# Norm sums as one column per token tile: root and reciprocal on four columns, spread over the partitions by products with the identity

## The reference

```python
def _rmsnorm(x, g):
    xf = x.astype(jnp.float32)
    y = xf * lax.rsqrt(jnp.mean(xf * xf, axis=-1, keepdims=True) + EPS)
    return (y * g.astype(jnp.float32)).astype(x.dtype)
...
        h = _rmsnorm(x, norm_g[l, 0]) * (1.0 + sc0) + sh0
        x = x + 0.5 * g0 * _swiglu(h, ffn_w_gate[l, 0], ffn_w_up[l, 0], ffn_w_down[l, 0])
        h = _rmsnorm(x, norm_g[l, 1]) * (1.0 + sc1) + sh1
...
        h = _rmsnorm(x, norm_g[l, 2]) * (1.0 + sc2) + sh2
```

## Time and profile before

| | us |
|---|---|
| median of 3 runs | 3887.87 |
| the runs | 3886.22, 3887.87, 3887.95 |
| profiled execution | 3886.95 |
| its span | 3885.2 |
| TensorE busy | 3486.6 (90%) |
| VectorE busy | 2174.4 (56%) |
| GpSimd busy | 1606.3 (41%) |
| ScalarE busy | 1216.5 (31%) |

### The profile page before, as it was taken

One profiled execution on the slowest core, in us unless ns is written; L12 is line 12 of the kernel. 1 busy time (PEld: TensorE's weight loads), 2 busy tenths in 40 slices (PEclk: granted clock), 3 DMA queues, 4 the chain that ended last, 5 costly groups with the idle time before them and its releaser, 6 DMA issues. The chain is left out here.

```text
span 3885.2 us, 41685 instructions
## 1 busy us (share of the span) xinstructions
PE 3486.6 (90%) x13886; PEld 2361.7 (61%) x13886; DVE 2174.4 (56%) x4271; ACT 1216.5 (31%) x2225; POOL 1606.3 (41%) x960
## 2 busy tenths in 40 slices
PE   6999999899999999999999999897778778777777
PEld 4888676688878887766788876663333333333332
DVE  6546257433326455466333265478677777667664
ACT  3332226443323323145333233432222222222221
POOL 3446330244545455210444632335444444444442
PEclk9999999999999999999999999998998998999998
DMA  6526320122435454200223421269999999999996
GB/s 243 194 95 259 110 98 1 45 97 97 166 126 184 146 201 179 98 17 16 88 97 112 179 82 49 93 255 408 421 422 421 421 421 422 421 421 421 420 420 275
DMA packets 141434, 839.57 MB, mean 216 GB/s; under 512 B 15824, under 2 KB 16464, under 8 KB 63952
## 3 DMA queue, kind: packets, MB, share of 16 engines
q0 software_dynamic: 73728, 536.90, 33.5%
q1 hardware_dynamic: 67536, 300.56, 21.5%
HBM read 835.31 MB, written 2.10 MB: 216 GB/s over the span
## 5 line engine op out<-in xcount | busy, mean ns | idle before, releaser
L256 POOL TENSOR_TENSOR wlo<-wraw,whi 128x1024 fp32r<-128x1024 f32 x357 | 906.2, 2543 | 1462.9 <-ACT whi L252 1462.6
L252 ACT ACTIVATE whi<-wraw 128x1024 fp32r<-128x1024 f32 x357 | 377.4, 1058 | 663.4 <-DMA wraw<-in_wts 371.8
L263 PE MATMUL f_ps<-f_hh,whi 128*128 128x512 f32 x1408 | 550.3, 391 | 0.9 <-DVE f_hl L352 0.9
L264 PE MATMUL f_ps<-f_hl,whi 128*128 128x512 f32 x1408 | 548.2, 389 | 0.0
L265 PE MATMUL f_ps<-f_hh,wlo 128*128 128x512 f32 x1408 | 548.1, 389 | 0.0
L1967 PE MATMUL g_psF<-g_low,g_diagb 128*128 128x512 f32 x660 | 327.6, 650 | 101.0 <-ACT g_diagb L2025 100.9
L1967 PE MATMUL g_psF<-g_own,g_diagb 128*128 128x512 f32 x576 | 279.8, 636 | 71.9 <-ACT g_diagb L2025 71.9
L521 DVE TENSOR_TENSOR f_a<-f_sg,f_ps 128x512 f32<-128x512 f32 x88 | 60.5, 688 | 503.6 <-PE f_ps L265 487.1
L1967 PE MATMUL g_psF<-g_top,g_diagb 128*128 128x512 f32 x524 | 261.8, 651 | 72.3 <-ACT g_diagb L2025 72.2
L1967 PEld LDWEIGHTS g_psF<-g_low,g_diagb 128*128 128x128 f32 x660 | 134.7, 208 | 288.9 <-issue 288.9
L2019 ACT ACTIVATE g_dotb<-g_dotb 128x4 f32<-128x4 f32 (+1 forms) x134 | 27.5, 205 | 898.4 <-DVE g_dotb L2109 898.4
(11 more groups left out here) (400 smaller groups left out, 6396.9 us busy)
## 6 DMA issues: line engine op xcount, KB each, us to landing
wraw<-in_wts SPq DMA_DIRECT2D x360, 512.0 KB, 3.3
m_wrow<-in_ada SPq DMA_DIRECT2D x52, 1024.0 KB, 6.8
m_erow<-in_ada SPq DMA_DIRECT2D x28, 1024.0 KB, 5.0
p_wt<-in_wtok SPq DMA_DIRECT2D x2, 3168.0 KB, 10.5
p_wt<-in_w SPq DMA_DIRECT2D x2, 3072.0 KB, 9.7
g_low<-in_uv,idx POOLq DMA_INDIRECT x165, 24.8
g_own<-in_uv,idx POOLq DMA_INDIRECT x144, 24.3
g_top<-in_uv,idx POOLq DMA_INDIRECT x131, 24.8
```

The source lines that it names most:

```text
L252: self.nc.scalar.activation(self.T.whi[:, j % 4], self.T.wraw[:, j % 2], ACT.Copy).then_inc(self.M["w_hi"], 1)
L256: self.nc.gpsimd.tensor_tensor(self.T.wlo[:, j % 4], self.T.wraw[:, j % 2], self.T.whi[:, j % 4].bitcast(F32), ALU.subtract).then_inc(self ...
L263: self.nc.tensor.matmul(out, hi, xh, start=first, stop=False)
L264: self.nc.tensor.matmul(out, hi, xl, start=False, stop=False)
```

## The change

The sums are turned round: the squares, 128 tokens at a time, are the stationary operand, and one column of the ones is the moving one. Four products give [128, 4]: token t*128+p has its mean square on partition p, column t. The root and the reciprocal are made on these four columns, in `T.root` and `T.inv`, which are unused columns of `T.eps`. `widen` then copies each of the four columns 128 times along the free dimension, in two copies of 256 columns, to the place of the old `T.rstd`, and `spread` multiplies these by the identity, four products of 128 columns, so that the [128, 512] form stands in a PSUM bank, `T.psN`. `norm_split` and its likes read that bank in place of `T.rstd`.

```diff
+def token_sums(nc, T, out, x, first, last):
+    for t in range(TT):
+        mm = nc.tensor.matmul(out[:, t:t + 1], x[:, t * P:(t + 1) * P], T.const[:, C_ONES:C_ONES + 1],
+                              start=first and t == 0, stop=last and t == TT - 1, skip_group_check=True)
+    return mm
+
+def widen(nc, T, dve, sem):
+    nc.vector.reciprocal(T.inv[:, :], T.root[:, :]).then_inc(sem, 1)
+    dve.wait_ge(sem, 1)
+    wide = T.wide[:, :].rearrange("p (t m) -> p t m", t=TT)
+    for a in range(2):
+        nc.vector.tensor_copy(wide[:, 2 * a:2 * a + 2], T.inv[:, 2 * a:2 * a + 2].unsqueeze(2).to_broadcast([P, 2, P])
+                              ).then_inc(sem, 1)
+
+def spread(nc, T, pe, sem, out):
+    for t in range(TT):
+        pe.wait_ge(sem, t // 2 + 2)
+        mm = nc.tensor.matmul(out[:, t * P:(t + 1) * P], T.wide[:, t * P:(t + 1) * P], T.const[:, C_IDENT:C_IDENT + P],
+                              start=True, stop=True, skip_group_check=True)
+    return mm
...
     def total(self, pe):
-        ones = self.T.const[:, C_ONES:C_ONES + P]
         pe.wait_ge(self.M["n_acc"], KD - 2)
-        self.nc.tensor.matmul(self.ps, ones, self.acc, start=True, stop=False)
+        token_sums(self.nc, self.T, self.ps, self.acc, True, False)
         pe.wait_ge(self.M["n_sq"], KD)
...
     def root(self, act):
         act.wait_ge(self.M["n_sum"], 1)
-        self.nc.scalar.activation(self.T.rstd[:, :], self.ps, ACT.Sqrt, ...
+        self.nc.scalar.activation(self.T.root[:, :], self.ps[:, 0:TT], ACT.Sqrt, ...
...
@@ norm_split
-                nc.vector.scalar_tensor_tensor(u[:, k % slots], T.xT[:, k], gain[:, k:k + 1], T.rstd[:, :],
+                nc.vector.scalar_tensor_tensor(u[:, k % slots], T.xT[:, k], gain[:, k:k + 1], T.psN[:, :],
...
@@ ffn
                 Q.total(pe)
-                keep_busy(nc, T, pe, psD[:, 0], 9, 256)
+                keep_busy(nc, T, pe, psD[:, 0], 4, P)
+                Q.spread(pe)
+                keep_busy(nc, T, pe, psD[:, 0], 4, 256)
...
@@ out_proj (and second_mix alike)
-                keep_busy(nc, T, pe, ps[:, 0], 4)
+                keep_busy(nc, T, pe, ps[:, 0], 4, P)
+                Q.spread(pe)
+                keep_busy(nc, T, pe, ps[:, 0], 4, 256)
```

More of the change, by code:

```diff
@@ L173, in _ @@
                 act.wait_ge(M["m_ch"], 3)
[L174 removed]
+                nc.scalar.activation(T.root[:, :], psN[:, 0:TT], ACT.Sqrt, bias=T.eps[:, 0:1]).then_inc(M["n_root"], 1)
                 for n in range(3):
@@ L190, in _ @@
                     pe.wait_ge(M["n_sq"], k + 1)
-                    nc.tensor.matmul(psN[:, :], T.const[:, C_ONES:C_ONES + P], sq[:, k % 2], start=k == 0,
-                                     stop=k == KD - 1).then_inc(M["n_sum"], 1)
+                    token_sums(nc, T, psN, sq[:, k % 2], k == 0, k == KD - 1).then_inc(M["n_sum"], 1)
+                spread(nc, T, pe, M["n_rstd"], psN)
                 pe.wait_ge(M["m_dot"], 2 * ROWS)
-                keep_busy(nc, T, pe, psN, 2)
+                keep_busy(nc, T, pe, psB, 2)
             @block.vector
@@ L207, in _ @@
                         dve.wait_ge(M["n_root"], 1)
-                        nc.vector.reciprocal(T.rstd[:, :], T.rstd[:, :]).then_inc(M["n_rstd"], 1)
+                        widen(nc, T, dve, M["n_rstd"])
                     dve.wait_ge(M["m_row"][j], 16)
@@ L318, in total, with spread @@
     def total(self, pe):
-        ones = self.T.const[:, C_ONES:C_ONES + P]
         pe.wait_ge(self.M["n_acc"], KD - 2)
-        self.nc.tensor.matmul(self.ps, ones, self.acc, start=True, stop=False)
+        token_sums(self.nc, self.T, self.ps, self.acc, True, False)
         pe.wait_ge(self.M["n_sq"], KD)
-        self.nc.tensor.matmul(self.ps, ones, self.sq[:, (KD - 1) % 2], start=False, stop=True).then_inc(self.M["n_sum"], 1)
+        token_sums(self.nc, self.T, self.ps, self.sq[:, (KD - 1) % 2], False, True).then_inc(self.M["n_sum"], 1)
     def root(self, act):
         act.wait_ge(self.M["n_sum"], 1)
-        self.nc.scalar.activation(self.T.rstd[:, :], self.ps, ACT.Sqrt, bias=self.T.eps[:, 0:1]).then_inc(self.M["n_root"], 1)
+        self.nc.scalar.activation(self.T.root[:, :], self.ps[:, 0:TT], ACT.Sqrt, bias=self.T.eps[:, 0:1]).then_inc(self.M["n_root"], 1)
     def rstd(self, dve):
         dve.wait_ge(self.M["n_root"], 1)
-        self.nc.vector.reciprocal(self.T.rstd[:, :], self.T.rstd[:, :]).then_inc(self.M["n_rstd"], 1)
+        widen(self.nc, self.T, dve, self.M["n_rstd"])
+    def spread(self, pe):
+        spread(self.nc, self.T, pe, self.M["n_rstd"], self.T.psN)
+def token_sums(nc, T, out, x, first, last):
[16 more added lines that the diff above has]
+    return mm
 N_SEMS = "n_u n_hi n_lo "
@@ L404, in ffn @@
         psD = ctx.enter_context(nc.psum_tensor("f_psD" + str(which), [P, 2, S], F32))
-        psN = ctx.enter_context(nc.psum_tensor("f_psN" + str(which), [P, S], F32))
         W = Stream(nc, T, M, layer * LAYER_T + (FFN_T + PROJ_T + OUT_T if which else 0))
-        Q = Sums(nc, T, M, a32[:, 0], sg, psN[:, :])
+        Q = Sums(nc, T, M, a32[:, 0], sg, T.psN)
         norm = (nc, T, M, sg, hh, hl, gain, shift)
@@ L1237, in out_proj @@
         ps = ctx.enter_context(nc.psum_tensor("o_ps", [P, 4, S], F32))
-        psN = ctx.enter_context(nc.psum_tensor("o_psN", [P, S], F32))
-        Q = Sums(nc, T, M, acc[:, :], sq, psN[:, :])
+        Q = Sums(nc, T, M, acc[:, :], sq, T.psN)
         with nc.Block() as block:
@@ L1503, in _ @@
                     pe.wait_ge(M["l_sq"], k + 1)
-                    nc.tensor.matmul(psT[:, 0], ones, sg[:, k % 2], start=k == 0, stop=k == KD - 1).then_inc(M["l_sum"], 1)
-                keep_busy(nc, T, pe, psT[:, 1], 4)
+                    token_sums(nc, T, psT[:, 0], sg[:, k % 2], k == 0, k == KD - 1).then_inc(M["l_sum"], 1)
+                keep_busy(nc, T, pe, psT[:, 1], 4, P)
+                spread(nc, T, pe, M["l_r"], T.psN)
+                keep_busy(nc, T, pe, psT[:, 1], 4, 256)
             @block.scalar
@@ L1610, in _ @@
                 act.wait_ge(M["l_sum"], KD)
-                nc.scalar.activation(T.rstd[:, :], psT[:, 0], ACT.Sqrt, bias=T.eps[:, 1:2]).then_inc(M["l_root"], 1)
+                nc.scalar.activation(T.root[:, :], psT[:, 0, 0:TT], ACT.Sqrt, bias=T.eps[:, 1:2]).then_inc(M["l_root"], 1)
             @block.gpsimd
@@ L1778, in _ @@
                 dve.wait_ge(M["l_root"], 1)
-                nc.vector.reciprocal(T.rstd[:, :], T.rstd[:, :]).then_inc(M["l_r"], 1)
+                widen(nc, T, dve, M["l_r"])
         clear(nc, M)
@@ L2193, in build @@
             T.rstd = cw.enter_context(nc.sbuf_tensor("rstd", [P, S], F32))
+            T.wide = T.rstd
+            T.root, T.inv = T.eps[:, 4:8], T.eps[:, 8:12]
             first_block(nc, T)
```

29 lines of the change are left out of this document (17 added, 12 removed).

## The result

The changed kernel takes 3900.42 us, median of 8 runs (3899.04 to 3902.98); the kernel before, on the same chip, 3886.68 us, median of 8 (3883.54 to 3889.91). The ratio is 1.0037, 95% interval 1.0028 to 1.0046: slower, by 13.7 us. The forecast was 3885.0, with a range up to 3892. The profiled run of after took 3901.13 with a span of 3898.6, 13.4 more than before's 3885.2. TensorE is busy for 3519.6 us of it, before for 3486.6.

What follows compares the result with a forecast made beforehand. TensorE, busy 90% of the span, was taken as the bound, its fills holding the barrier at norms. Six norms 2.6, second_mix 0.3 + 0.1 and first_modulation 0 gave 3.0 us less than 3887.87: 3885, range 3878 to 3892.

Steps and rivals of the forecast that it cites:

- a clock fall inside the chain: Rival: TensorE drops to 1.2 GHz after the sums, 3.2 us more at four of seven norms: 3899; chance 0.12.
- The step that failed: Argument against the clock fall: narrow stretch half as long as in soft_attention, idle 0.72 not 1.50, full fills at once.
- second_mix: Norm ending this stage: 0.3 us less at its end, and 0.1 from the alternation of ScalarE and TensorE before it.
- its eight records (0.98) fill the 7.70 / 8 = 0.96 that a turn takes now: In second_mix, one product's narrow records fill a turn, though 0.14 us less from start to end; 0.1 gain taken.
- first_modulation: First norm: copies may wait until GpSimd pauses, so dots start where they did: 0 gain, otherwise up to about 1.1 us.
- The price of every small operation: Along a norm's chain: sums 0.98 us, root 0.31, reciprocal 0.20, each copy about 0.30, spread 1.11, last fills 1.89.
- The barrier: At block ends it waits for TensorE's fills: TensorE ends last at 4.80 against 5.24 us, 0.44 less at six norms.
- The rival that the fills don't hold the barrier: Blocks end with the spread: 2.17 us less at six norms, 2.03 at second_mix, 15.0 in all: 3872.9; chance 0.08.
- VectorE's readers of PSUM: 64 VectorE operations read PSUM in place of SBUF, 0.743 against 0.747 us in the rows: no cost.
- The rule of the Trainium skill, VectorE: DVE Perf Modes (the TRN2 errata): Rival on PSUM reads: some 0.065 us more each, 4.1 over 64: 3889; chance 0.10 shared with slow small operations.
- The copies under GpSimd: In first_modulation, copies at 36.6 may stand until GpSimd pauses at 38.66, leaving the following dots where they were.
- the sum of the prediction: Whole kernel: 2.6 + 0.3 + 0.1 + 0 = 3.0 us less, forecast 3885; chance 0.60.

Runs made afterwards that it cites:

- r1_after_again: The changed kernel timed and traced once more, with no edit: 3901.72 us, ratio to before 1.0036.
- e1_wide_ones: Changed kernel with 128 equal columns of ones, not one, as the sums' moving operand: 3884.01 us, ratio to before 0.9994.
- e7_before_fill_1col: Kernel before, the nine 256-column fills at the ends of ffn replaced by sixteen of one column: 3887.72 us, ratio 1.0002.
- e8_before_fill_128col: Kernel before, the nine 256-column fills at the ends of ffn replaced by sixteen of 128 columns: 3887.87 us, ratio 0.9997.
- e4_wide_no_last: Changed kernel with 128 columns of ones in the sums and no fills behind the spread: 3870.01 us, ratio to before 0.9957.
- e9_wide_ends_only: Changed kernel with 128 columns of ones in first_modulation and second_mix only: 3893.06 us, ratio to before 1.0012.
- e2_no_last_fill: Changed kernel without the four 256-column fills behind the spread in ffn, out_proj and second_mix: 3883.20 us, ratio to before 0.9993.
- e3_gap_fill: Changed kernel with one 512-column fill between the two groups of narrow sums in ffn and out_proj: 3890.72 us, ratio to before 1.0012.
- e6_wide_no_fill: Changed kernel with 128 columns of ones and no fills ahead of or behind the spread: 3869.90 us, ratio to before 0.9955.
- e5_before_narrow: Kernel before, four of the nine fills at the ends of ffn replaced by eight one-column products: 3886.48 us, ratio 0.9998.

## Why the prediction was wrong

I had priced the rival that came true, a clock fall inside the chain, at 3899, and gave it 0.12.

**The step that failed** is the weighing of that rival. I argued that "here the narrow stretch is half as long", that the idle time before it is 0.72 and not 1.50, and that "full fills follow at once". The first is false by the change itself: the accumulated tiles' sums are narrow too. The timeline shows two groups of eight one-column records, 411.94 and 413.69, as many as the 16 of `soft_attention`, with 0.80 of idle time in between, and the four first fills behind them have 128 columns, not 512., the one row of before on what TensorE's clock does after such records, showed 0.50, and I reasoned it away. What came instead was a fall to 0.50 at five of the seven norms, and at all seven in `r1_after_again`. After against `e1_wide_ones` shows the cause, the first end of `e7_before_fill_1col` against `e8_before_fill_128col` supports it, and `r1_after_again` shows that the place varies.

**The rival's price** came out right in part by chance. I had 3.2 more than before for each fallen norm. Measured are 6.88 - 5.65 = 1.2 at each `ffn`: the clock falls at 415.88 (the 0.97 of the stretch from 414 to 416), behind the first fills, so that 16 records and not 24 are left, and it reads 0.68 in the last stretch, on its way back. The rest came from terms that I had not seen. The stages of the four traces (from a stage's start to the next one's, in us, to about 0.1) sum up to the spans:

| | before | after | `e1_wide_ones` | `e4_wide_no_last` |
|---|---|---|---|---|
| `first_modulation` | 46.5 | 47.9 | 45.9 | 47.2 |
| four `ffn` | 1492.6 | 1498.8 | 1490.5 | 1483.5 |
| two `proj_mix` | 331.0 | 332.2 | 332.2 | 330.0 |
| two `soft_attention` | 275.5 | 275.4 | 273.7 | 275.4 |
| two `out_proj` | 107.4 | 108.4 | 108.1 | 105.2 |
| `second_mix` | 215.3 | 219.7 | 213.4 | 213.4 |
| `peer` | 1416.9 | 1416.2 | 1414.2 | 1413.5 |
| span | 3885.2 | 3898.6 | 3878.0 | 3868.2 |

(The profiled execution of `e1_wide_ones` was the fastest of its 11, 3880.27 against a median of 3884.01, so its column is not typical.) Of after's 13.4, the ends of `ffn` are 4 x 1.23 = 4.9, the ends of `out_proj` -0.8, the squares and the end of `second_mix` 2.8 + 2.7 = 5.5, `first_modulation` 1.4, together 11.0. The other 2.4 lie elsewhere: in the starts of stages, in `second_mix` ahead of its squares (-1.2) and in `peer` (-0.7). A start at the low clock costs: four fills took 1.96 in before and 3.64 in after at 422.59. These starts differ between traces of one kernel as well (a slow `out_proj` start costs 0.9), and no run of mine isolates them; what of the 2.4 belongs to the change stays open.

**`second_mix`** was forecast at 0.4 less and was 4.4 more; its squares and its end alone cost 5.5. The step "its eight records (0.98) fill the 7.70 / 8 = 0.96 that a turn takes now" held at the full clock alone: at the low one they take 1.71. With wide ones the 64 records took 7.87 (`e1_wide_ones`, `e4_wide_no_last` and `e9_wide_ends_only` alike), 0.17 more than before where I had 0.1 less, and the block ended 5.40 after the last square, 0.4 sooner. The stage of `e1_wide_ones` is 1.9 shorter than before, but 1.7 of that lie ahead of its first square, and in `e4_wide_no_last` they are not there.

**`first_modulation`** I gave 0, having looked only at the copies. The sums there were not costed, and they are on the path. Its timeline in after, and the queue that finished last:

```profile
21.13 13.81 PE L341 MATMUL psN<-const,m_sq 128*128 128x1 f32 x64 [21.13 <-DMA const<-in_const]
...
34.98 0.26 ACT L175 ACTIVATE eps<-psN,eps 128x4 f32<-128x4 f32 x1 [1.48 <-PE psN L341]
35.14 1.99 ACT L178 ACTIVATE whi<-wraw 128x1024 fp32r<-128x1024 f32 x2
...
43.77 2.34 POOL L184 TENSOR_TENSOR wlo<-wraw,whi 128x1024 fp32r<-128x1024 f32 x1 [1.17 <-ACT whi L178]
```

```profile
L144 POOLq DRAIN  x1: 2441/2441/2441, 43.7 to 43.7; - x1
```

13.81 for the sums, 9.31 before and 10.28 in `e1_wide_ones`. ScalarE's rounding stands behind the root in its queue, GpSimd's rest behind the rounding, and its third tile ends last: 1.4 more for the stage. The view prints a granted clock of 1.00 here in every trace. It is not to be trusted so early: in `e1_wide_ones` the count of records in 2 us goes from 11 to 20 with the printed clock unchanged, in after it stays at 11. First the two stretches of `e1_wide_ones`, then those of after:

```profile
22.00:24.00 2.00, 2.00 (x11) 2.00 (x11) 0.74 (x3) 0.63 (x1) 0.00 (x0) 1.00 1.02 426
27.00:29.00 2.00, 2.00 (x20) 1.98 (x19) 1.77 (x4) 1.34 (x3) 0.00 (x0) 1.00 1.06 422
```

```profile
22.00:24.00 2.00, 2.00 (x11) 2.00 (x11) 0.74 (x3) 0.63 (x1) 0.00 (x0) 1.00 1.02 426
27.00:29.00 2.00, 2.00 (x11) 2.00 (x11) 1.82 (x4) 0.71 (x2) 0.00 (x0) 1.00 1.04 416
```

The 11 records in 2 us are also the count in `second_mix` at 0.50. The traces' own clock events begin with a rise to 1.00: at 26.73 in `e1_wide_ones`, the moment at which the pace doubles, and at 40.42 in after, behind the sums. So the stage begins at the low clock, and under the one-column sums TensorE stays there for 13.81 us, busy all the time. The four traces with narrow sums in this stage (after, `r1_after_again`, `e2_no_last_fill`, `e3_gap_fill`) all show 13.81, the four with wide ones 9.06 to 10.28.

**What was right.**

- The price of every small operation: sums 1.05 (0.98 forecast), root 0.26 (0.31), reciprocal 0.18 (0.20), each copy 0.29 (0.30), spread 1.16 at full clock (1.11), last fills 1.89 (1.89). Where the clock held in after, at `out_proj`, TensorE ended 4.88 after the last square and the block 5.23: 0.42 less than before, where I had 0.44.
- The barrier. TensorE's DRAIN is the last row, VectorE's ends 4.4 earlier in after, and in `e1_wide_ones`, at full clock, 2.7 (forecast: 2.6). The rival that the fills don't hold the barrier is out: `e4_wide_no_last` had to take them out to reach 3870.01, near the 3872.9 of that rival.
- VectorE's readers of PSUM cost nothing (line 380, in ns):

```profile
L380 DVE SCALAR_TENSOR_TENSOR f_sg<-xT,gain,psN x32: 739/748/750, 48.3 to 1899.3; 128x512 f32<-128x512 f32 x32
L380 DVE SCALAR_TENSOR_TENSOR y<-xT,gain,psN x16: 737/742/748, 422.5 to 1540.5; 128x512 f32<-128x512 f32 x16
```

With T.rstd in SBUF it was 0.747. The rule of the Trainium skill, VectorE: DVE Perf Modes (the TRN2 errata), by which the prediction had estimated 4.1 us in all, does not show here.

- The copies under GpSimd. In after they came at 35.49, before GpSimd began at 36.27, and took 0.49 for both. In `e1_wide_ones`, where the earlier sums put them into GpSimd's time:

```profile
32.75 6.01 POOL L184 TENSOR_TENSOR wlo<-wraw,whi 128x1024 fp32r<-128x1024 f32 x2 [32.22 <-ACT whi L178]
...
36.69 2.42 DVE L352 COPY rstd<-eps 128x256 f32<-128x256 f32 x2
```

They took 2.42 and ended 0.35 after GpSimd paused, at 38.76, as the prediction had it. The Trainium skill, GPSIMD Engine Reference (SBUF interfaces), names contention between GpSimd and VectorE for some forms of VectorE's instructions; the trace agrees in that the copies waited, but no run here shows in which form they ran.

So the sum of the prediction was that of another kernel: `e1_wide_ones`, in which the clock holds, took 3884.01 where 3885 had been forecast for the change. It and before can't be told apart (0.9985 to 1.0003): 3.2 us of VectorE's chain taken out at seven norms shorten each block by 0.3 to 0.4, and that is too little for the times to show, as long as fills hold the barrier. The full gain comes when both are done, sums with 128 columns and no fills behind the spread: 3870.01, 17 us below before, the fastest here with `e6_wide_no_fill`. That the forecast fits `e1_wide_ones` is in part luck too: `second_mix` ahead of its squares and the starts of stages move by more between traces than the 3.0 us that were forecast.

## What to carry to other kernels

Work given to TensorE to keep its clock must be long enough to cover the wait and no longer: once the wait is shortened, the barrier waits for the work instead (a DRAIN of 2.65 with the fills, 0.97 without). Products with one moving column cost nearly as much time as those with 128 when each loads its own weights (3.63 and 3.73 for 32 records at the full clock), and they are the ones under which the clock fell; so pad the moving operand where PSUM has room. And when a trace of before holds one row of the kind of work that a change adds, take the clock in that row as the forecast until a run speaks against it; arguments on length and idle time, made without a row, were what failed here.

## What the runs showed of the hardware that I had not expected

- The granted clock can fall from 1.00 to 0.50 while TensorE is busy without a gap, if its records have one moving column: 32 such records took 5.65 us at one end of `ffn` and 3.63 at the other three, where the fall came at their end or behind it; 32 with 128 columns took 3.73 at all four.
- Nor does it rise under them: at the start of the program 64 records of one column took 13.81 us in each of four traces, 0.21 a record, and the first rise came after them; with 128 columns the pace doubled on the way, at 24.0 to 26.7.
- The fall is not the same each time: none at `out_proj` in one trace of after and both in another; two of four in `e5_before_narrow`. One product of 512 columns between the two groups of narrow ones held the clock at six norms of six.
- In `second_mix` of the changed kernel the narrow sums at 0.50 pace the squares, and the clock came back only among the last fills, 14 us after the fall, in both of its traces.
- A copy that repeats 2 values over 256 columns takes 0.29 us on VectorE; one that started with GpSimd at work took 2.22 us.
